# Two key blocks' probabilities added before one transpose, in the local attention of a two-layer transformer

## The reference

```
q, z = split(h @ w_in)                       # 32 query heads of 64, 4 key/value heads
logits = einsum("bnqkgd,bnskd->bnkgqs", q, k_band) + bias    # query block n sees key blocks n-1 and n
logits = where(mask, logits, -inf)           # 0 <= dist = qi + 128 - s < 128
m = max(max(logits), sink)
p = exp(logits - m)
probs = p / (sum(p) + exp(sink - m))
o = probs @ v_band
o = o * silu(z); out = o @ w_out
```

## Time and profile before

| | |
|---|---|
| median of 3 runs | 1538.3 us (1535.33, 1538.30, 1538.49) |
| profiled execution | 1535.09 us, span 1533.3 us |
| mean granted TensorE clock | 0.999 |
| TensorE busy | 1514.9 us, 99% |
| TensorE weight loads | 1215.5 us, 79% |
| VectorE busy | 920.2 us, 60% |
| ScalarE busy | 735.1 us, 48% |
| GpSimd busy | 257.6 us, 17% |

### The profile page before, as it was taken

The page is one execution under the profiler, slowest core; times in us unless marked ns, Lnnn a source line. Parts: engine busy times, 40 slices in busy tenths (PEclk is TensorE's granted clock), DMA queues, the critical chain, the costliest instruction groups (busy, mean ns, idle before and its releaser), DMA issues.

```text
span 1533.3 us, 20596 instructions
## 1 busy us (share of the span) xinstructions
PE 1514.9 (99%) x7592; PEld 1215.5 (79%) x7592; DVE 920.2 (60%) x1733; ACT 735.1 (48%) x1284; POOL 257.6 (17%) x446
## 2 busy tenths in 40 slices
PE   9999999999999999999999999999999999999998
PEld 7878888888888877877886887666678888888887
DVE  5767777787654466666768435554375243433467
ACT  4454455544553356555667324566555241322343
POOL 2044334444402003433341000000000000000000
PEclk9999999999999999999999999999999999999999
DMA  5321111111114332222321232112223223232321
GB/s 206 110 70 56 56 56 56 55 56 56 56 56 142 110 102 87 83 70 69 90 83 56 85 111 75 56 57 67 69 81 105 90 97 111 84 108 91 102 83 69
DMA packets 40163, 127.21 MB, mean 83 GB/s; under 512 B 4576, under 2 KB 9104, under 8 KB 40064
## 3 DMA queue, kind: packets, MB, share of 16 engines
q1 hardware_dynamic: 38112, 121.65, 24.1%
q0 software_dynamic: 1040, 3.27, 0.6%
q10 hardware_dynamic: 912, 0.99, 0.2%
...
## 4 chain that ended last, share of the span: by engine, by line
PE 93%; DVE 3%; ACT 3%; issue 1%; DMA 0%; POOL 0%; SPq 0%; DVEq 0%; ACTq 0%; POOLq 0%
PE ps L883 90%; PE ps L1260 2%; PE ps L1028 1%; ACT L L1817 1%; DVE wl L2015 1%; DVE L L2557 0%; ACT sp L1911 0%; DVE up L2169 0%; ACT sp L1909 0%; DMA wraw<-in_wa 0%; ACT sp L1913 0%; ACT xr L1849 0%; DVE qkv L2053 0%; DVE xr L2606 0%; DVE U L2367 0%
## 5 line engine op out<-in xcount | busy, mean ns | idle before, releaser
L883 PE MATMUL ps<-xr,wh 128*128 128x512 f32 x2720 | 871.5, 401 | 1.5 <-DVE xr L2606 0.7
L883 PEld LDWEIGHTS ps<-xr,wh 128*128 128x128 f32 x2720 | 499.0, 188 | 124.2 <-issue 27.0
L883 PE MATMUL ps<-xr,wl 128*128 128x512 f32 x1376 | 537.8, 391 | 0.0
L2015 DVE TENSOR_TENSOR wl<-wraw,wh 128x1024 fp32r<-128x1024 f32 x214 | 261.5, 1229 | 134.4 <-ACT wh L1404 133.3
L883 PEld LDWEIGHTS ps<-xr,wl 128*128 128x128 f32 x1376 | 258.3, 188 | 55.7
L1404 ACT ACTIVATE wh<-wraw 128x1024 fp32r<-128x1024 f32 x214 | 222.0, 1048 | 74.5 <-PE ps L883 73.0
L883 PE MATMUL ps<-xm,wh 128*128 128x512 f32 x640 | 197.7, 390 | 0.0
L883 PEld LDWEIGHTS ps<-xm,wh 128*128 128x128 f32 x640 | 119.5, 188 | 26.3 <-DVE xm L2692 1.6
L883 PE MATMUL ps<-xm,wl 128*128 128x512 f32 x320 | 124.6, 389 | 0.0
L2866 POOL TENSOR_SCALAR L<-L,m 128x256 f32<-128x256 f32 (+1 forms) x120 | 90.4, 771 | 193.7 <-DVE m L2572 193.7
L2053 DVE SCALAR_TENSOR_TENSOR qkv<-cin,gains,qkv 128x512 f32<-128x512 f32 x96 | 85.6, 892 | 9.7 <-ACT qkv L1434 8.9
...
## 6 DMA issues: line engine op xcount, KB each, us to landing
...
```

The costliest lines, as they stand in the source:

```text
L883: return e.matmul(out, w, x, start=start, stop=stop, skip_group_check=True)
L2015: e.tensor_tensor(m.wl[:, i % N_SPLIT, :], m.raw[:, i % N_RAW, :], m.wh[:, i % N_SPLIT, :].bitcast(F), ALU.subtract).then_inc(s.wlo, 1)
```

## The change

- GpSimd adds `L[..., 0:128]` to `L[..., 128:256]` for n = 1, 2, 3 (both heads in one instruction, 2 x 128 elements), when the exponentials of n are done, ahead of the denominators. As one of the two is zero at every place, nothing is lost.
- Scaling is of 128 columns for every n.
- TensorE transposes only columns 128:256: 2 per n, 8 per j.
- VectorE writes `pT[n]` for n = 1, 2, 3: the transposed square, read twice, times two triangles (`band`, made once by GpSimd in `masks`). ScalarE copies n = 0.
- ScalarE's silu and its table loads move behind the copy of n = 0.
- Signal counts follow: `pr` grows by `MERGED` = 3 per j, `bz` by 2. For j >= 14 VectorE's scaling waits for the additions.
- `PLAN` is written anew for b, b14, b15, c0 to c3.

```diff
-    return 8 * min(j, SHARED) + 4 * max(j - SHARED, 0)
+    return (MERGED + 8) * min(j, SHARED) + (MERGED + 4) * max(j - SHARED, 0)
...
-    "b": plan("x13 b0 b0 a0 a3 b0 b0 a0 b0 a0 b1 a0 b0 b0 b0 a0 a1 a0 a0 b0 a0"),
-    "b14": plan("x7 b2 b0 b2 b0 a0 a3 b0 b0 a0 a1 a1 a6 b5 a4 b0 b0 a1 a0"),
+    "b": plan("x10 b1 b1 a0 a0 b5 b0 a0 a0 b0 b0 b0 b0 a1 a0 b0 a0 a0 a0 a0 b0"),
+    "b14": plan("x6 b0 b1 b4 b0 a1 a2 b5 a0 a1 b3 a0 b5 a0 b0 a0 b3 a1 a0"),
...
-    "b15": plan("x3 b0 b0 b9 b4 b0 b0 b0 b2 b0"),
+    "b15": plan("x6 b0 b5 b1 b3 b0 b1 b0 b2 b0"),
...
 TensorE, attend2
-                e.wait_ge(s.pr, scaled_by_pool(j) + 2 * n + 2)
-            for kb in ((0, 1) if n else (1,)):
-                for ee in range(2):
-                    ins = e.transpose(m.bk(b)[:, 2 * kb + ee, :], m.L[:, c, ee, n, kb * 128:(kb + 1) * 128], m.flip[:])
+                e.wait_ge(s.pr, scaled_by_pool(j) + MERGED + 2 * n + 2)
+            for ee in range(2):
+                ins = e.transpose(m.bk(b)[:, ee, :], m.L[:, c, ee, n, 128:256], m.flip[:])
             ins.then_inc(s.tr_p, 1)
-            clear[b] = [((s.pT_v, s.pT_a)[n % 2], 2 * j + n // 2 + 1)]
+            clear[b] = [(s.pT_v, 3 * j + n)] if n else [(s.pT_a, j + 1)]
...
 ScalarE, attend2
-        if j % 2:
-            for jj in (j - 1, j):
-                ... silu of z
-            if j < 15:
-                tables()
         for n in range(4):
             b = turned()
-            if n % 2:
+            if n == 0:
                 ...
-                e.activation(m.pT[:, n, :], m.bk(b), ACT.Copy).then_inc(s.pT_a, 1)
+                e.activation(m.pT[:, 0, 2:4], m.bk(b)[:, 0:2], ACT.Copy).then_inc(s.pT_a, 1)
+            if n == 1 and j % 2:
+                ... silu of z for j - 1 and j, then tables() if j < 15
...
 VectorE, attend
+            e.wait_ge(s.pr, scaled_by_pool(j) + MERGED)
             for u in range(4, 8):
-                x = m.L[:, c, u % 2, u // 2, :]
+                x = m.L[:, c, u % 2, u // 2, 128:256]
...
 VectorE, attend2
-            if n % 2 == 0:
-                k0 = 0 if n else 2
+            if n:
                 ...
-                e.tensor_copy(m.pT[:, n, k0:], m.bk(b)[:, k0:]).then_inc(s.pT_v, 1)
-            elif n == 1 and j % 2:
+                e.tensor_tensor(m.pT[:, n].rearrange("p (k e) c -> p k e c", k=2),
+                                m.bk(b)[:, 0:2, :].unsqueeze(1).to_broadcast([128, 2, 2, 128]),
+                                m.band.unsqueeze(2).to_broadcast([128, 2, 2, 128]), ALU.mult).then_inc(s.pT_v, 1)
+            if n == 1 and j % 2:
                 gated(j - 1)
...
 GpSimd, begin_b
+        e.tensor_tensor(m.band[:, 0, :], m.ones, m.triu, ALU.subtract).then_inc(s.bz, 1)
+        e.tensor_copy(m.band[:, 1, :], m.triu).then_inc(s.bz, 1)
         e.memset(m.vz[:], 0.0).then_inc(s.bz, 1)
...
 GpSimd, attend
         yield from idle(8)
+        for n in range(1, 4):
+            x = m.L[:, c, :, n, 128:256]
+            e.wait_ge(s.ex, 8 * j + 2 * n + 2)
+            e.tensor_tensor(x, x, m.L[:, c, :, n, 0:128], ALU.add).then_inc(s.pr, 1)
         e.wait_ge(s.den, denominators(j) + 2)
```

More of the change, by code:

```diff
@@ L282 @@
 SHARED = 14
+MERGED = 3
 def scaled_by_pool(j):
-    return 8 * min(j, SHARED) + 4 * max(j - SHARED, 0)
+    return (MERGED + 8) * min(j, SHARED) + (MERGED + 4) * max(j - SHARED, 0)
 def denominators(j):
@@ L305 @@
     "b-": plan("x13 a1 a1 a0 a0 a0 a1 a2 a0 a0"),
-    "b": plan("x13 b0 b0 a0 a3 b0 b0 a0 b0 a0 b1 a0 b0 b0 b0 a0 a1 a0 a0 b0 a0"),
-    "b14": plan("x7 b2 b0 b2 b0 a0 a3 b0 b0 a0 a1 a1 a6 b5 a4 b0 b0 a1 a0"),
-    "c0": plan("x0 s0 s7 s8 s0 s0 s11 s0 s2 s3 s0 s0 s1 s0 s2"),
-    "c1": plan("s0 s6 s5 x2 s0 s11 s0 s0 s0 s6 s0 s0 s0 s1 s5"),
-    "c2": plan("x1 s0 s8 s4 s3 s5 s0 s0 s5 s2 s0 s0 s1 s0 s6"),
-    "c3": plan("x2 s2 s2 s3 s1 s2 s0 s1 s0 s2 s0 s0 s1 s0 s3"),
-    "b15": plan("x3 b0 b0 b9 b4 b0 b0 b0 b2 b0"),
+    "b": plan("x10 b1 b1 a0 a0 b5 b0 a0 a0 b0 b0 b0 b0 a1 a0 b0 a0 a0 a0 a0 b0"),
+    "b14": plan("x6 b0 b1 b4 b0 a1 a2 b5 a0 a1 b3 a0 b5 a0 b0 a0 b3 a1 a0"),
+    "c0": plan("s0 s0 x8 s6 s1 s2 s8 s0 s2 s4 s0 s0 s1 s0 s2"),
+    "c1": plan("s0 s6 s7 s1 s1 s8 s0 s2 s0 x6 s0 s0 s1 s0 s4"),
+    "c2": plan("x1 s1 s6 s5 s2 s5 s0 s0 s0 s9 s0 s0 s1 s0 s5"),
+    "c3": plan("x2 s3 s0 s3 s0 s0 s3 s0 s3 s1 s0 s0 s1 s0 s3"),
+    "b15": plan("x6 b0 b5 b1 b3 b0 b1 b0 b2 b0"),
 }
@@ L626, in __init__ @@
         self.bias = b.new([2, 2, 256], name="bias")
+        self.band = self.masks[:, 0:2, :]
         loff = b.p
@@ L1268, in attend2 @@
             e.wait_ge(s.vz, 4)
-        e.wait_ge(s.pT_v, 2 * j + 2)
-        e.wait_ge(s.pT_a, 2 * j + 2)
+        e.wait_ge(s.pT_v, 3 * j + 3)
+        e.wait_ge(s.pT_a, j + 1)
         for n in range(4):
@@ L1768, in begin_b @@
     def begin_b():
-        e.wait_ge(s.bz, 1)
+        e.wait_ge(s.bz, 3)
         e.activation(m.blk1r[:], m.blk1, ACT.Copy).then_inc(s.hn_hi, 1)
@@ L1810, in attend @@
         if j >= 2:
-            e.wait_ge(s.pr, 8 * (j - 2) + 8)
+            e.wait_ge(s.pr, scaled_by_pool(j - 1))
         for n in range(4):
@@ L1825, in attend2 @@
     def attend2(j):
-        if j % 2:
-            for jj in (j - 1, j):
-                e.wait_ge(s.z, jj + 1)
-                e.activation(m.XF[:, 16 + jj, :], m.XF[:, 16 + jj, :], ACT.Silu).then_inc(s.zs, 1)
-            if j < 15:
-                tables()
         for n in range(4):
             b = turned()
-            if n % 2:
-                e.wait_ge(s.tr_p, 4 * j + n + 1)
+            if n == 0:
+                e.wait_ge(s.tr_p, 4 * j + 1)
                 if j:
-                    e.wait_ge(s.pv_p, 4 * (j - 1) + n + 1)
-                e.activation(m.pT[:, n, :], m.bk(b), ACT.Copy).then_inc(s.pT_a, 1)
+                    e.wait_ge(s.pv_p, 4 * (j - 1) + 1)
+                e.activation(m.pT[:, 0, 2:4], m.bk(b)[:, 0:2], ACT.Copy).then_inc(s.pT_a, 1)
+            if n == 1 and j % 2:
+                for jj in (j - 1, j):
+                    e.wait_ge(s.z, jj + 1)
+                    e.activation(m.XF[:, 16 + jj, :], m.XF[:, 16 + jj, :], ACT.Silu).then_inc(s.zs, 1)
+                if j < 15:
+                    tables()
             yield
@@ L2860, in attend @@
         yield from idle(8)
+        for n in range(1, 4):
+            x = m.L[:, c, :, n, 128:256]
+            e.wait_ge(s.ex, 8 * j + 2 * n + 2)
+            e.tensor_tensor(x, x, m.L[:, c, :, n, 0:128], ALU.add).then_inc(s.pr, 1)
         e.wait_ge(s.den, denominators(j) + 2)
         for n in range(2 if j >= SHARED else 4):
-            lo = 0 if n else 128
+            if n:
+                e.wait_ge(s.pr, scaled_by_pool(j) + n)
             for ee in range(2):
-                x = m.L[:, c, ee, n, lo:]
+                x = m.L[:, c, ee, n, 128:256]
                 e.tensor_scalar(x, x, m.den[:, c, 2 * n + ee:2 * n + ee + 1], 1.0, ALU.mult,
@@ L2938, in kv_post @@
             if n == 0:
-                e.wait_ge(s.bz, 2)
+                e.wait_ge(s.bz, 4)
             e.wait_ge(s.hn, n + 1)
```

2 lines of the change are left out of this document (added).

## The result

| | before | after |
|---|---|---|
| median, us | 1536.9 (6 runs, 1535.3 to 1538.5) | 1541.9 (6 runs, 1540.6 to 1545.0) |
| profiled execution, span | 1535.09, 1533.3 | 1545.03, 1543.1 |
| mean granted TensorE clock | 0.999 | 0.994 |

The ratio is 1.0039, 95% between 1.0029 and 1.0049: the change makes the kernel slower, by about 6 us (5.0 between the medians). I had forecast 5.9 us less. The profiled execution of after is the slowest of its six.

A forecast was written before the change was run, and what follows sets the result against it. TensorE's own work was taken to bound the attention. Gains of 0.7 (first head), 5.2 (steady heads) and 0 (last two) summed to 5.9 us: 1529.2 profiled, 1532.4 from the median; range 1524 to 1539.

The forecast's parts named there:

- Part 1: TensorE, local attention: 96 transposes removed at 0.12 us each, 0.72 us per head, 11.5 us in all (bounds 10.6 and 13.2).
- Part 3: GpSimd's additions, sharing ports with VectorE, delay scalings; n = 0 transposes stall 0.32 us, net gain 0.40 per steady head, 5.2 us.
- Part 5: First and last heads: j = 0 gains 0.7 us; j = 14 and 15 together zero, 3 us to either side.
- Part 2: TensorE's n = 0 transposes move four steps earlier, to 9.47 us; period 16.38 if inputs ready, but second scaling ends at 9.45.
- Part 4: VectorE's masked products (0.69 us each) and ScalarE's moved silu cost nothing, with cover of 0.1 us in odd heads.
- (C): Rival: a second wait, for the n = 2 scalings, costs 0.3 to 0.4 us per head; gain 1.4 us, 1536.9; chance 0.15.
- (D): Rival: slower, since a GpSimd addition costs 1.0 us and not 0.7; 0.3 us lost per head, 1543; chance 0.13.

The follow-up runs named there:

- e10: From e7, silu again behind ScalarE's n = 0 copy, and VectorE's gating of head j - 1 moved to its queue's end in odd heads; 1529.1 us, ratio 0.9950.
- e5: Kernel after with each GpSimd addition on 2 of 128 columns, so its output is not the layer's; 1534.2 us, ratio 0.9986.
- e11: Kernel after with GpSimd's third addition (n = 3) moved behind the scalings of n = 0 to 2, heads 0 to 13; 1536.1 us, ratio 0.9996.
- e6: Kernel before with only the new TensorE order of the steady heads (plan b); 1545.1 us, ratio 1.0053.
- e1: Kernel after with all seven TensorE orders (b, b14, b15, c0 to c3) of the kernel before; 1539.9 us, ratio 1.0024.
- e7: Kernel after with all old orders, silu at its old place, and heads 0, 14 and 15 unmerged as in the kernel before; 1532.9 us, ratio 0.9981.
- e8: Kernel after with all old orders, and ScalarE's silu and table loads back at their old place; 1537.9 us, ratio 1.0013.
- e3: Kernel after with only the orders of the last two heads (b14, b15) of the kernel before; 1543.7 us, ratio 1.0044.
- e4: Kernel after with only the orders c0 to c3 of the kernel before; 1543.4 us, ratio 1.0047.
- e12: e8 with unread 512-column products put ahead of TensorE's waits in the last two heads; 1535.9 us, ratio 0.9996.

## Why the prediction was wrong

In short: 5.9 us of gain were forecast and 6.3 of loss measured, 12.2 apart, and three terms failed. Part 1 gave a head 0.72 us for its transposes where 0.48 came, 3.1 us over thirteen heads. Part 3 took 0.32 us for the stall where 0.48 came, 2.1 us, because it had no term for the denominator that waits for an addition. Part 5 put the first head at a gain of 0.7 and the last two at zero, with nothing for the clock behind a wait of TensorE, where 6.3 us were lost: 7.0 us, the largest.

**Part 1, the worth of a transpose.** The number is 96, as said, and the price was at the lower of my bounds. The groups of one head before (the next start behind each is that of the scores):

```profile
685.49 0.82 PE L1260 MATMUL ps<-flip,L 128*128 128x128 f32 x6
686.24 0.93 PE L883 MATMUL ps<-kpad,qb 64*128 64x128 f32 x8
...
689.28 1.03 PE L1260 MATMUL ps<-flip,L 128*128 128x128 f32 x8
690.24 1.13 PE L883 MATMUL ps<-kpad,qb 64*128 64x256 f32 x7
```

and of one head of e10, with VectorE's masked products of the same head:

```profile
667.15 0.60 PE L1277 MATMUL ps<-flip,L 128*128 128x128 f32 x4
667.68 0.93 PE L900 MATMUL ps<-kpad,qb 64*128 64x128 f32 x8
...
670.76 0.60 PE L1277 MATMUL ps<-flip,L 128*128 128x128 f32 x4
671.29 1.13 PE L900 MATMUL ps<-kpad,qb 64*128 64x256 f32 x8
672.57 1.75 PE L900 MATMUL ps<-pT,vz 128*64 128x128 f32 x28
```

```profile
671.18 1.29 DVE L2629 TENSOR_TENSOR pT<-ps,masks 128x512 f32<-128x512 f32 x2 [0.96 <-PE ps L1277]
```

Six and eight took 0.75 + 0.96 = 1.71 us; four and four take 0.53 + 0.53 = 1.06. That is 0.65 for six, 0.11 each. My upper value, 0.137, came from a group with a wait in it, and I should not have moved towards it. But a head doesn't get the 0.65. In e10 the V product starts 1.28 us after the second scores and not 1.06, right where VectorE's second masked product ends (672.47): 0.2 us go to this. In e5, with the order of after, the eight stand as four lone pairs with small gaps around them. Its period is 0.47 us shorter than before, so these pairs cost 1.71 - 0.47 = 1.24 us, 0.16 each, if nothing else in the head changed; this is an estimate. The period itself fell by 0.47 to 0.50 us a head in the three kernels without a listed wait of TensorE in the steady heads (e5, e11, e10), where I had forecast 0.72.

**Part 2, the place.** The place at 9.47 was nearly right: in e5, without a wait, it is 9.62, so 0.15 of the delay to 10.03 is not GpSimd's. The doubt about the place was right too. e6 shows that the scalings themselves would have been in time.

**Part 3, the stall.** Its place and its releaser were right; the size, 0.25 to 0.5 with 0.32 taken, was 0.40 to 0.42 as a wait and 0.48 as time. An addition takes 0.75 us where I had 0.7, so that was no error; my chain gave it only 0.6, against that price, and still had the end of the third nearly right (7.85 forecast, 7.81 measured). What I passed over in half a sentence ("if the small denominator instructions get between"), and named again only among the signs, was the decisive case, and it happens in every head. I let the additions be delayed by VectorE, but not an instruction of eight elements by an addition. This pushed the reciprocal from about 7.6 to 8.1, and with it the question who wins, L2018 or the first scaling, was settled: L2018 wins by 0.09 us, and the first two scalings are over at 9.9. I had priced this branch right (9.85 to 9.9) and took a value between the two branches, where there was nothing to average. The Trainium skill (SBUF — State Buffer, SBUF: two separate sides) had the rule of the exclusive lock and the trace agrees: a VectorE instruction with two SBUF inputs goes from 0.17 to 0.64 us beside an addition. Net per head: 0.40 forecast, 0.72 - 0.32; measured 0.48 - 0.48, nothing.

**Part 4.** VectorE's product is 686 ns, forecast 0.69, and TensorE has no listed wait for it in the steady heads of after. But where n = 2 and 3 are turned in one group, in e10, two such products in a row hold the V product by 0.2 us (Part 1). And the cover that I gave to odd heads, 0.1 us, is there only with the new order: e1, with the old one, loses 1.06 us in each odd head to the gating that waits for the moved silu. With the silu at its old place (e7, e8) it is 0.6 us, now at ScalarE's n = 0 copy. "Costs nothing" held, by the order that goes with it.

**Part 5, the ends.** Here are all the 6.3 us, 1.3 in the first head and 5.0 in the last two with equal work. The first head: 0.7 us of gain forecast. "Its transposes are not late" is true and was not enough: the same late denominator delays VectorE's squares, for which TensorE there already waited 1.66 us. The wait grew by 0.46. Counted with equal work (0.69 off), e5 and e11, whose denominator has its old length and whose wait is 1.62 and 1.65, take 17.4 us against 17.86, a gain of 0.5. e3 and e4, with the longer wait and a full clock, take 17.8 to 17.9, no gain. After, with the longer wait and the clock fallen, takes 19.2. So the wait costs about 0.5 us every time, and the clock another 1.3 in those executions in which it falls.

The last two heads: I had forecast waits of 1.7 to 2 us in j = 14 and set them off against a gain in j = 15. The wait came, 2.04. A second of 1.32 and a third of 2.09 came with it, and the lower clock in the windows around them. The step that failed is this zero: nothing in j = 15 paid for the waits, and the clock had no term. e7 shows that leaving these heads unmerged gives it all back; e12 that half or more of e8's loss there is clock.

**The rivals.** By the total it is none of them. The steady heads came out near (C), 0.05 us a head against 0.0 measured, but by one wait and a smaller net gain, not by a second wait at n = 2. (D)'s time, 1543, is near that of after, but additions of 1.0 us didn't occur. What none had was a loss in the three heads that aren't steady. I had given these "3 us to either side", and that a wait of 2 us can take the clock with it was not in any of my terms.

**What stays open.** Why the clock fell at 427 to 436 in some executions of unchanged code, and why behind the wait of 2.1 us in the first head it fell in three profiled executions and held in four. How the 1.24 us of the lone pairs splits into transposes and gaps. And I did not run e11's order together with e7's unmerged ends, which by the table should come near e10.
